# Expert weights of two MoE layers loaded in runs of 16 KB and 8 KB instead of 4 KB

## The chip, the cores and the metric

The kernel runs on one NeuronCore of a Trainium2 chip. Its time is the device time of one execution in microseconds (us). The kernel before was timed in 3 runs: 2659.59, 2661.01 and 2648.42 us, with a median of 2659.59.

A core has five engines that run side by side and wait for each other by semaphores: TensorE (PE, matmuls and transposes; its weight loads are shown as PEld), VectorE (DVE), ScalarE (ACT), GpSimd (POOL) and SyncE (SP), which here only issues transfers. Transfers between the device memory and the on-chip memory (SBUF, 128 partitions) are carried out by 16 DMA engines.

## The reference

Three blocks of a transformer run one after the other on x with 256 tokens and 1,024 features, all in fp32. The second has two layers, each ending in a mixture of experts; this is the part that the change touches:

```python
# in the block, for layer i; mc are the six conditioning vectors of the layer
    ... + mc[5] * ec_moe(modulate(rms_norm_2(hc, norm2_g[i]), mc[3], mc[4]), *moe)

def ec_moe(h, w_r, w_gate, w_up, w_down):
    ...
    aff = jax.nn.softmax(jnp.einsum("bnd,de->bne", h, w_r).astype(jnp.float32), axis=-1)
    gates, idx = lax.top_k(jnp.swapaxes(aff, 1, 2), cap)      # 32 tokens for each of 16 experts
    ...
    xs = h[bidx, idx]
    hid = jax.nn.silu(jnp.einsum("becd,edf->becf", xs, w_gate)) * jnp.einsum("becd,edf->becf", xs, w_up)
    ys = jnp.einsum("becf,efd->becd", hid, w_down) * gates[..., None].astype(h.dtype)
    return jnp.zeros_like(h).at[bidx, idx].add(ys)
```

The three matrices of an expert are 1024 x 1024, 4 MB each, so the two layers read 2 x 16 x 12 MB = 403 million bytes of expert weights, of 634 million that the kernel moves in all.

## The kernel before

All weights of the kernel pass through a ring of 6 slots of 16 KB per partition (`ring`, `RING = 6`). `weight_chunks` lists the chunks in the order of their use. SP takes the list in order: before it loads a chunk into a slot it waits until PE has used the chunk that was there, and each slot has a semaphore (`landed`) for PE to wait on.

An expert is six chunks of 2 MB: `g0 g1 u0 u1 d0 d1`, the upper and lower 512 rows of gate, up and down. In `rows_of` the 512 rows of a chunk are split as (k p): partition p gets rows p, 128 + p, 256 + p and 384 + p, each 4 KB long. A transfer is therefore 512 runs of 4 KB, four per partition.

Each MoE layer goes like this:
- Its input is normalised (`norm_act` for the first 128 tokens on ScalarE, `norm_dve` for the others on VectorE, lines L357 and L365) and stands in `xn`, tokens on partitions. PE turns it into `hT` for the router (L1519), and the 32 tokens of each expert are gathered out of `xn` by matmuls with one-hot columns (L1545), 128 features at a time, into `xsT` (128 features x tokens, 8 such tiles), where scale and shift are applied.
- A loop over expert pairs follows. For each expert PE waits for a slot, multiplies with the chunks of gate and up (L1571, 32 small matmuls on a chunk), ScalarE and VectorE make `hid` (L1504, L1475), PE transposes it (L1578), ScalarE copies it out (L1506), PE multiplies with the two down chunks (L1587), ScalarE copies the result to `ys` (L1508), and PE adds it to the output tokens by matmuls with the scatter matrix (L1594).
- In each matmul the feature (or hidden) number on the partitions of the small operand has to be the row number of the weights on the same partition.
- In SP's program the loads of expert 0 are issued ahead of the loop (L2175), as soon as their slots are free. `load_moe` then holds a loop over the others: `part` waits on `moe_used` for the slot and issues a 2 MB transfer whose expert number is in a register (L2191, L2193).

The vectors of the conditioning (`ada_w_2`) are computed as rows of 512 features and turned to columns, 128 features at a time, by `ada_columns_pe` (L816), 24 chunks in all; they and the gains of the norms (`cols`) are features on partitions.

Of the kernel before, what the change touches and what calls it, by code (L numbers as in the profile page):

```python
# [119 lines left out]
def offsets(table):  # L120
    at, out = 0, {}
    for name, n in table:
        out[name] = (at, n)
        at += n
    return out, at


COL_AT, N_COLS = offsets(COLS)
ROW_AT = [offsets(t) for t in ROWS]
N_ROWS = max(n for _, n in ROW_AT)  # L130

# [40 lines left out]
    return w[k0 * P:k1 * P, c0:c1].rearrange("(k p) n -> p k n", p=P)  # L172


def weight_chunks(A):


# [5 lines left out]
    def whole(name, w, k0, k1, c0, c1):  # L183
        chunk(name, k1 - k0, c1 - c0, (0, rows_of(w, k0, k1, c0, c1)))
# [26 lines left out]
    def moe(l):  # L211
        for e in range(N_EXPERTS):
            for what, w in (("g", "moe_w_gate_2"), ("u", "moe_w_up_2"), ("d", "moe_w_down_2")):
                for h in range(2):
                    whole(f"moe{l}_{e}{what}{h}", A[w][l, e], 4 * h, 4 * h + 4, 0, 1024)

    ev = A["ev_w_in_2"][0]
    whole("ev_kv", ev, 0, 8, 512, 768)
# [32 lines left out]
def program(nc, A, out, planned):  # L251
# [12 lines left out]
    with ctx:  # L264
# [37 lines left out]
        def constant(name, p=P):  # L302
            at, n = CONST_AT[name]
            return const[0:p, at:at + n]
# [43 lines left out]

        def norm_act(tag, ready):

            a = nc.scalar
            waits(a, *ready)
            a.activation(xn[:, 0, :], x[:, 0, :], ACT.Square, accum_out=stats[:, 0:1]).then_inc(*act_s.signals(f"{tag}.ss0"))  # L355
            a.wait_ge(*pool_s.after(f"{tag}.rstd0"))
            a.activation(xn[:, 0, :], x[:, 0, :], ACT.Copy, scale=stats[:, 4:5]).then_inc(*act_s.signals(f"{tag}.xn0"))  # L357

        def norm_dve(tag):
            v = nc.vector  # L360
            v.wait_ge(*dve_s.latest())
            v.tensor_tensor_reduce(out=xn[:, 1, :], in0=x[:, 1, :], in1=x[:, 1, :], scale=1.0, scalar=0.0,
                                   op0=ALU.mult, op1=ALU.add, accum_out=stats[:, 1:2]).then_inc(*dve_s.signals(f"{tag}.ss"))
            v.wait_ge(*pool_s.after(f"{tag}.rstd"))
            v.tensor_scalar(xn[:, 1, :], x[:, 1, :], stats[:, 5:6], None, ALU.mult).then_inc(*dve_s.signals(f"{tag}.xn1"))  # L365

        def normed(tag):
            return [(act_s, f"{tag}.xn0"), (dve_s, f"{tag}.xn1")]
# [441 lines left out]
        def ada_columns_pe(c):  # L810
            t_ = nc.tensor
            _, at, row_ = ada_place(c)
            t_.wait_ge(*act_s.after(f"ada.c{c}"))
            claim(at)
            for b in range(4):
                ins = t_.matmul(bank[at][:, 2 * b:2 * b + 2], row_[:, P * b:P * b + P], constant("ada_cols"),  # L816
                                start=True, stop=True, skip_group_check=True)
            ins.then_inc(*pe_s.signals(f"ada.e{c}"))
            lend(at, (dve_s, f"ada.m{c}"))
# [585 lines left out]

        def moe_pool(l):
            waits(nc.gpsimd, ((act_s, "ln silu"), (dve_s, "moe0.x3"))[l])
            nc.gpsimd.dma_start(w_r, A["moe_w_r_2"][l].rearrange("(k p) e -> p k e", p=P)).then_inc(s_side2["w_r"], 16)
            norm_pool(f"nmoe{l}")

        def moe_dve(l):
            v = nc.vector
            tag = f"moe{l}"
            norm_dve(f"nmoe{l}")
            turn_evac(f"h{tag}", h2_items[l], 1)

            v.memset(s_buf[:, 0, :], 0.0).then_inc(*dve_s.signals(f"{tag}.zeros"))
# [68 lines left out]
        def moe_act(l):  # L1486
            a = nc.scalar
            tag = f"moe{l}"
            norm_act(f"nmoe{l}", [(dve_s, ("ev_out1.x0", "sc_out1.x0")[l])])
            turn_evac(f"h{tag}", h2_items[l], 0)  # L1490
            a.wait_ge(*dve_s.after(f"{tag}.max"))
            for t in range(2):
# [17 lines left out]
        def moe_pe(l):  # L1510
# [39 lines left out]
            with t_.Fori(0, N_EXPERTS // 2) as i:  # L1550
                for b in range(2):
# [23 lines left out]
                    t_.wait_ge(moe_hid, done + 1)  # L1575
                    t_.wait_ge(moe_hTc, done)
                    for h in range(2):
                        ins = t_.transpose(bank[5][:, P * h:P * h + P], hid[b][:, P * h:P * h + P], ident)  # L1578
                    ins.then_inc(moe_hT, 1)
                    t_.wait_ge(moe_hTc, done + 1)  # L1580
                    t_.wait_ge(moe_yc, done)
# [590 lines left out]
        def load_plain(sp, name):  # L2172
            n, kt, width, pieces = chunks[name]
            for c0, src in pieces:
                sp.dma_start(slot(name)[:, :, c0:c0 + src.shape[2]], src).then_inc(landed[n % RING], 16)  # L2175
# [4 lines left out]
        def load_moe(sp, l):  # L2180

            parts = moe_parts(l)
            first = chunks[parts[0]][0]
            for c in range(RING):
                sp.wait_ge(*pe_s.after(f"used {names[first + c - RING]}"))
                load_plain(sp, parts[c])

            def part(c, i, expert):
                w = A[("moe_w_gate_2", "moe_w_up_2", "moe_w_down_2")[(c % 6) // 2]][l]
                s = (first + c) % RING  # L2190
                sp.wait_ge(moe_used, 12 * i + (96 * l + c + 1))  # L2191
                src = w[bass.ds(expert, 1), 512 * (c % 2):512 * (c % 2) + 512, :].rearrange("e (k p) n -> p (e k) n", p=P)
                sp.dma_start(ring[:, s, :].rearrange("p (k n) -> p k n", n=D), src).then_inc(landed[s], 16)  # L2193

            with sp.Fori(0, N_EXPERTS // 2 - 1) as i:
                for c in range(12):
                    part(c, i, 2 * i + (1 + c // 6))
            for c in range(6):
                part(c, N_EXPERTS // 2 - 1, N_EXPERTS - 1)
# [89 lines left out]
```

## Time and profile before

| | |
|---|---|
| median of 3 runs | 2659.59 us (2648.42 to 2661.01) |
| profiled execution: span from first to last instruction | 2661.3 us; the page names no time outside it |
| PE busy | 2127.6 us, 80% |
| DVE, ACT, POOL busy | 599.1, 342.2, 120.5 us |
| DMA | 634.34 MB, mean 238 GB/s |
| packets of SP's queue | 251,536, 623.83 MB |
| chain that ended last | PE 63%, DMA 28%, DVE 4% |

The profile is of one execution. Its page splits the span into 40 slices of 66.5 us and gives the busy share of each engine in tenths. The chain of waits goes back from the last instruction, at each step to what released it. A line like L1571 is a line of the kernel before. DMA share is the mean busy share of the 16 DMA engines; it can pass 1, because packets that follow each other on one engine overlap a little in the record.

### The profile page before, as it was taken

Reading aid. Unit: us, or ns where it says so; the run is one execution under the profiler, and the core shown is the slowest. Engines: PE = TensorE matmul, PEld = TensorE weight load, DVE = VectorE, ACT = ScalarE, POOL = GpSimd, SP = SyncE. Lnnn points to the kernel's source line nnn. Section 1 sums busy time; section 2 is a strip of 40 time slices with the busy share of each in tenths; the row PEclk is TensorE's granted clock in tenths of the full one; section 3 lists DMA queues with packets and bytes.
Section 4 is the critical chain, followed back from the end, with each engine's and each line's share of the span. In section 5 each row is a group of like instructions: output and inputs, shape, how many; then the busy total and the mean of one; then the engine's idle time right before and its main releaser. Section 6 shows DMA issues by size and latency. Waiting matters only on the chain.

```text
span 2661.3 us, 30350 instructions
## 1 busy us (share of the span) xinstructions
PE 2127.6 (80%) x12671; PEld 1258.4 (47%) x12671; DVE 599.1 (23%) x1662; ACT 342.2 (13%) x802; POOL 120.5 (5%) x154
## 2 busy tenths in 40 slices
PE   8999999898655555589855555549989999979999
PEld 3455545574322222267422222224558764446874
DVE  2223203673000000022300000012623421242330
ACT  1034211031000000010100000001311100211110
POOL 0100000530000000000000000001100000000000
PEclk9987699858888888889888888888979999959999
DMA  9767463301899999995299999996223434403430
GB/s 344 253 215 267 159 228 129 127 1 64 356 410 410 410 410 410 410 246 190 109 409 410 409 410 410 410 404 228 95 79 128 158 112 158 142 16 116 144 135 16
DMA packets 256024, 634.34 MB, mean 238 GB/s; under 512 B 7394, under 2 KB 89458, under 8 KB 255945
## 3 DMA queue, kind: packets, MB, share of 16 engines
q1 hardware_dynamic: 251536, 623.83, 62.7%
q0 software_dynamic: 1472, 5.76, 0.6%
q10 hardware_dynamic: 2936, 3.66, 0.4%
q8 instruction: 54, 0.88, 0.1%
q14 instruction: 26, 0.21, 0.0%
HBM read 632.13 MB, written 1.09 MB: 238 GB/s over the span
## 4 chain that ended last, share of the span: by engine, by line
PE 63%; DMA 28%; DVE 4%; SPq 2%; ACT 1%; issue 1%; POOL 1%; POOLq 0%; DVEq 0%; ACTq 0%
PE bank L538 20%; DMA ring<-in_moe_w_down 17%; PE bank L553 15%; DMA ring<-in_moe_w_gate 10%; PE bank L1909 6%; PE bank L596 3%; PE bank L618 3%; PE bank L1587 2%; PE bank L805 2%; SPq L2193 2%; PE bank L609 2%; PE bank L1571 2%; PE bank L464 1%; PE bank L1545 1%; PE bank L816 1%
## 5 line engine op out<-in xcount | busy, mean ns | idle before, releaser
L1571 PE MATMUL bank<-ring,arena 128*32 128x256 f32 x4096 | 306.4, 453 | 251.6 <-DMA ring<-in_moe_w_up 150.2
L553 PE MATMUL bank<-hT,ring 128*128 128x256 f32 x1920 | 423.2, 384 | 4.3 <-DVE arena L1950 3.0
L538 PE MATMUL bank<-ring,hT 128*128 128x512 f32 (+3 forms) x992 | 418.3, 581 | 8.8 <-DVE hT L490 3.8
L553 PEld LDWEIGHTS bank<-hT,ring 128*128 128x128 f32 x1920 | 370.0, 193 | 57.2 <-issue 6.1
L1571 PEld LDWEIGHTS bank<-ring,arena 128*32 128x32 f32 x4096 | 141.2, 126 | 401.9 <-DMA ring<-in_moe_w_up 187.3
L538 PEld LDWEIGHTS bank<-ring,hT 128*128 128x128 f32 x992 | 188.2, 194 | 226.8 <-issue 223.6
L1587 PE MATMUL bank<-ring,arena 128*32 128x256 f32 x2048 | 165.2, 479 | 108.9 <-DMA ring<-in_moe_w_down 107.9
L1587 PEld LDWEIGHTS bank<-ring,arena 128*32 128x32 f32 x2048 | 78.0, 133 | 182.3 <-DMA ring<-in_moe_w_down 102.6
L1909 PE MATMUL bank<-ring,arena 128*128 128x512 f32 x352 | 151.4, 592 | 0.0
L1475 DVE TENSOR_TENSOR arena<-arena,bank 128x256 f32<-128x256 f32 x32 | 13.5, 421 | 557.2 <-ACT arena L1504 557.2
L1909 PEld LDWEIGHTS bank<-ring,arena 128*128 128x128 f32 x352 | 66.9, 190 | 83.3 <-issue 83.2
L419 POOL TENSOR_SCALAR stats<-stats 128x1 f32<-128x1 f32 (+7 forms) x40 | 7.8, 195 | 2011.0 <-ACT xn L355 1400.3
L538 PE MATMUL bank<-ring,arena 128*128 128x512 f32 (+1 forms) x224 | 92.5, 574 | 1.1 <-DVE arena L488 1.1
L1504 ACT ACTIVATE arena<-bank 128x256 f32<-128x256 f32 x32 | 12.3, 383 | 594.1 <-PE bank L1571 594.1
L1473 DVE COPY arena<-bank 128x256 f32<-128x256 f32 x32 | 13.6, 424 | 321.9 <-PE bank L1563 321.7
L618 PE MATMUL bank<-arena,pT_buf 128*128 128x64 f32 (+1 forms) x408 | 82.4, 346 | 0.0
L618 PEld LDWEIGHTS bank<-arena,pT_buf 128*128 128x128 f32 x408 | 81.4, 278 | 0.4 <-ACT pT_buf L641 0.2
L1961 DVE TENSOR_SCALAR arena<-arena,cols 128x256 f32<-128x256 f32 x88 | 30.4, 408 | 204.7 <-ACT arena L1932 204.7
L596 PE MATMUL bank<-arena 64*128 64x256 f32 (+2 forms) x144 | 67.6, 595 | 5.9 <-DVE arena L1842 3.1
L1964 DVE SCALAR_TENSOR_TENSOR arena<-arena,cols 128x256 f32<-128x256 f32 x176 | 71.5, 477 | 0.0
L538 PEld LDWEIGHTS bank<-ring,arena 128*128 128x128 f32 x224 | 43.4, 195 | 48.6 <-issue 47.5
L805 PE MATMUL bank<-ring,rows 128*32 128x512 f32 x384 | 65.5, 817 | 0.0
(285 smaller groups left out, 1700.1 us busy)
## 6 DMA issues: line engine op xcount, KB each, us to landing
ring<-in_moe_w_gate SPq DMA_DIRECT2D x64, 2048.0 KB, 23.6
ring<-in_moe_w_up SPq DMA_DIRECT2D x64, 2048.0 KB, 23.8
ring<-in_moe_w_down SPq DMA_DIRECT2D x64, 2048.0 KB, 23.9
ring<-in_ada_w SPq DMA_DIRECT2D x24, 2048.0 KB, 8.5
ring<-in_w_up SPq DMA_DIRECT2D x44, 1024.0 KB, 6.9
ring<-in_w_in SPq DMA_DIRECT2D x11, 2048.0 KB, 9.3
ring<-in_w_down SPq DMA_DIRECT2D x10, 2048.0 KB, 7.8
ring<-in_w_out SPq DMA_DIRECT2D x6, 2048.0 KB, 8.2
```

The costliest lines, as they stand in the source:

```text
L538: ins = t_.matmul(bank[b][:, 0:n], lhsT(k)[:, P * t:P * t + P], w[:, k, c0:c0 + n], start=(k == 0), stop=(k == kt - 1))
L553: ins = t_.matmul(bank[b][:, 256 * (j % 2):256 * (j % 2) + 256], w[:, k, P * j:P * j + P], rhs[:, k, :], start=(k == 0), stop=(k == 7), sk ...
L596: t_.matmul(score_bank(i)[:, 0:u["keys"]], u["q"], u["k"], start=True, stop=True)\
L609: ins = t_.transpose(bank[6 + j % 2][0:n, P * k:P * k + P], p[:, P * k:P * k + n], ident)
L618: ins = t_.matmul(bank[j % 2][:, 0:v.shape[-1]], pT_buf[0:n, j % 2, P * k:P * k + P], v, start=(k == 0), stop=(k == len(u["v"]) - 1))
L805: ins = t_.matmul(bank[b][32 * j:32 * j + 32, :], spad[:, j + 4 * r, :], w[:, j + 4 * r, :], start=(r == 0), stop=(r == 1), skip_group_che ...
L1571: ins = t_.matmul(bank[4][32 * j:32 * j + 32, at:at + 256], xs_now[b][:, 4 * (c % 2) + k, :], w[:, k, 256 * j:256 * j + 256], start=(c % 2 ...
L1587: ins = t_.matmul(bank[6][32 * j:32 * j + 32, 0:256], hidT[b][:, f % 2, 32 * (f // 2):32 * (f // 2) + 32], w[:, k, 256 * j:256 * j + 256], ...
L1909: ins = t_.matmul(bank[b][:, :], actT[:, f, P * t:P * t + P], w[:, k, 512 * half:512 * half + 512], start=(f == 0), stop=(f == FF_TILES - 1))
L1961: ins = v.tensor_scalar(dst, src, w, col("conv_b_3", 44 * l + f), ALU.mult, ALU.add)
L1964: ins = v.scalar_tensor_tensor(out=dst, in0=src, scalar=w, in1=dst, op0=ALU.mult, op1=ALU.add)
L2193: sp.dma_start(ring[:, s, :].rearrange("p (k n) -> p k n", n=D), src).then_inc(landed[s], 16)
```

## The change

The runs in which expert weights are loaded get longer, and everything that is multiplied with them is numbered to match:
- A gate or up chunk is split as (p k) instead of (k p): partition p gets rows 4p to 4p + 3 of the 512, which lie side by side in memory, 16 KB. A down chunk is split as (j p r): partition p gets rows 2p and 2p + 1 of each 256, two runs of 8 KB.
- The norm ahead of a MoE layer writes `xn` with its features in the matching order, reading `x` in steps of 4 elements.
- The router's weights, the columns of norm2_g, and the conditioning vectors 3 and 4 (bias and computed value) take the same order. For the computed value, `ada_columns_pe` reads its row in steps of 4; for the others the order is set in the load or in the array of columns.
- The two halves of `hid` that are transposed are its even and odd columns instead of its left and right half.

```diff
+def expert_order(a):
+    return a.reshape(-1, 2, P, 4).transpose(0, 1, 3, 2).reshape(-1, P)
+
+def expert_rows(w, what):
+    if what == "d":
+        return w.rearrange("(j p r) n -> p j (r n)", j=2, r=2)
+    return w.rearrange("(p k) n -> p (k n)", k=4)
+
+def expert_slot(slot, what):
+    return slot.rearrange("p (j n) -> p j n", j=2) if what == "d" else slot
...
-                    whole(f"moe{l}_{e}{what}{h}", A[w][l, e], 4 * h, 4 * h + 4, 0, 1024)
+                    chunk(f"moe{l}_{e}{what}{h}", 4, 1024, (None, expert_rows(A[w][l, e, 512 * h:512 * h + 512], what)))
...
+        def in_order(buf, t, experts):
+            if not experts:
+                return buf[:, t, :]
+            return buf[:, t, :].rearrange("p (h q k) -> p h k q", h=2, k=4)
+
+        def in_tiles(buf, t, experts):
+            return buf[:, t, :].rearrange("p (h k q) -> p h k q", h=2, k=4) if experts else buf[:, t, :]
...
-            a.activation(xn[:, 0, :], x[:, 0, :], ACT.Copy, scale=stats[:, 4:5]).then_inc(*act_s.signals(f"{tag}.xn0"))
+            a.activation(in_tiles(xn, 0, experts), in_order(x, 0, experts), ACT.Copy, scale=stats[:, 4:5]).then_inc(*act_s.signals(f"{tag}.xn0"))
...
-            v.tensor_scalar(xn[:, 1, :], x[:, 1, :], stats[:, 5:6], None, ALU.mult).then_inc(*dve_s.signals(f"{tag}.xn1"))
+            v.tensor_scalar(in_tiles(xn, 1, experts), in_order(x, 1, experts), stats[:, 5:6], None, ALU.mult).then_inc(*dve_s.signals(f"{tag}.xn1"))
...
-                ins = t_.matmul(bank[at][:, 2 * b:2 * b + 2], row_[:, P * b:P * b + P], constant("ada_cols"),
+                of = row_[:, b:512:4] if c % 12 // 2 in (3, 4) else row_[:, P * b:P * b + P]
+                ins = t_.matmul(bank[at][:, 2 * b:2 * b + 2], of, constant("ada_cols"),
...
-            nc.gpsimd.dma_start(w_r, A["moe_w_r_2"][l].rearrange("(k p) e -> p k e", p=P)).then_inc(s_side2["w_r"], 16)
+            nc.gpsimd.dma_start(w_r.rearrange("p (h k) e -> p h k e", h=2), A["moe_w_r_2"][l].rearrange("(h p k) e -> p h k e", h=2, k=4)).then_inc(s_side2["w_r"], 16)
...
-                        ins = t_.transpose(bank[5][:, P * h:P * h + P], hid[b][:, P * h:P * h + P], ident)
+                        ins = t_.transpose(bank[5][:, P * h:P * h + P], hid[b][:, h:256:2], ident)
...
-                src = w[bass.ds(expert, 1), 512 * (c % 2):512 * (c % 2) + 512, :].rearrange("e (k p) n -> p (e k) n", p=P)
-                sp.dma_start(ring[:, s, :].rearrange("p (k n) -> p k n", n=D), src).then_inc(landed[s], 16)
+                src = w[bass.ds(expert, 1), 512 * (c % 2):512 * (c % 2) + 512, :]
+                if what == "d":
+                    src = src.rearrange("e (j p r) n -> p (e j) (r n)", j=2, r=2)
+                else:
+                    src = src.rearrange("e (p k) n -> p (e k n)", k=4)
+                sp.dma_start(expert_slot(ring[:, s, :], what), src).then_inc(landed[s], 16)
```

No instruction changes its place on any engine: each engine issues the same number of the same operations in the same order, and only their access patterns differ. On SP, in the loop over the experts, the transfers of the first expert of a pair stood like this before (partitions x runs x elements):

```order
L2193 DMA ring<-in_moe_w_gate 128x4x1024
L2191 REGISTER_ALU
L2193 DMA ring<-in_moe_w_up 128x4x1024
L2191 REGISTER_ALU
L2193 DMA ring<-in_moe_w_down 128x4x1024
```

And in the changed kernel:

```order
L2238 DMA ring<-in_moe_w_gate 128x4096
L2232 REGISTER_ALU
L2238 DMA ring<-in_moe_w_up 128x4096
L2232 REGISTER_ALU
L2238 DMA ring<-in_moe_w_down 128x2x2048
```

Nothing moved; four runs of 1,024 elements per partition have become one of 4,096, or two of 2,048.

## Rows read from the trace of the kernel before

**Rows 1.** The page's 40 slices: PE, the DMA engines, and GB/s.

```profile
PE   8999999898655555589855555549989999979999
DMA  9767463301899999995299999996223434403430
GB/s 344 253 215 267 159 228 129 127 1 64 356 410 410 410 410 410 410 246 190 109 409 410 409 410 410 410 404 228 95 79 128 158 112 158 142 16 116 144 135 16
```

**Rows 2.** Stretches: length, busy us (xcount) of PE, PEld, DVE, ACT, POOL; PEclk, DMA share, GB/s.

```profile
672.39:1137.01 464.62, 266.26 (x3306) 127.61 (x3298) 20.67 (x79) 27.00 (x54) 0.00 (x0) 0.84 1.02 408
1316.31:1781.17 464.86, 254.85 (x3306) 122.98 (x3298) 20.67 (x79) 26.99 (x54) 0.00 (x0) 0.89 1.02 408
1785.00:1800.00 15.00, 0.00 (x0) 0.00 (x0) 10.83 (x15) 3.45 (x5) 4.45 (x10) 0.65 1.05 387
1140.00:1150.00 10.00, 5.57 (x52) 4.52 (x48) 6.49 (x10) 1.83 (x4) 0.92 (x3) 0.96 1.10 288
30.00:40.00 10.00, 10.00 (x24) 3.64 (x24) 1.59 (x5) 1.17 (x2) 0.00 (x0) 1.00 1.09 352
```

**Rows 3.** The chain that ended last, in the first loop: start us, us, what.

```profile
737.64 3.28 PE bank L1587 x32
...
744.63 23.69 DMA ring<-in_moe_w_down
768.36 3.27 PE bank L1587 x32
```

**Rows 4.** PE's waits, 672.39 to 1137.01: us in total, times, longest us.

```profile
PE bank L1571 <- DMA ring<-in_moe_w_up: 76.9, 30, 3.4
PE bank L1587 <- DMA ring<-in_moe_w_down: 52.0, 29, 3.1
PE bank L1571 <- DMA ring<-in_moe_w_gate: 42.1, 14, 3.0
PE bank L1578 <- DVE arena L1475: 15.1, 16, 1.0
```

**Rows 5.** DMA queues (packets, MB, share), and issues (KB each, us to landing).

```profile
q1 hardware_dynamic: 251536, 623.83, 62.7%
q8 instruction: 54, 0.88, 0.1%
...
ring<-in_moe_w_gate SPq DMA_DIRECT2D x64, 2048.0 KB, 23.6
```

**Rows 6.** Timeline of the second loop: start us, us, engine, line, operation [idle before <-releaser].

```profile
1366.49 3.42 PE L1571 MATMUL bank<-ring,arena 128*32 128x256 f32 x32 [3.19 <-DMA ring<-in_moe_w_up]
...
1371.61 1.93 PE L1571 MATMUL bank<-ring,arena 128*32 128x256 f32 x32 [1.70 <-DMA ring<-in_moe_w_up]
...
1374.97 0.38 ACT L1506 ACTIVATE arena<-bank 128x256 f32<-128x256 f32 x1 [0.98 <-PE bank L1578]
1376.73 3.42 PE L1587 MATMUL bank<-ring,arena 128*32 128x256 f32 x32 [1.79 <-DMA ring<-in_moe_w_down]
```

**Rows 7.** Timeline of SP at the start of the first loop.

```profile
672.39 2.08 SPq L2193 DMA_DIRECT2D ring<-in_moe_w_gate  x2
...
698.73 9.75 SPq L2193 DMA_DIRECT2D ring<-in_moe_w_up  x2
```

**Rows 8.** Single lines: duration ns min/median/max, first and last start us.

```profile
L1578 PEld LDWEIGHTS bank<-const,arena x64: 137/141/144, 678.3 to 1773.9; 128*128 128x128 f32 x64
...
L816 PEld LDWEIGHTS bank<-const,arena x192: 186/192/338, 92.5 to 388.5; 128*128 128x128 f32 x192
...
L365 DVE TENSOR_SCALAR xn<-x_sb,stats x10: 752/752/754, 11.7 to 2422.4; 128x1024 f32<-128x1024 f32 x10
...
L362 DVE CUSTOM_DVE_ANT_0 xn<-x_sb x10: 1224/1225/1226, 5.8 to 2420.2; 128x1024 f32<-128x1024 f32 x10
```

**Rows 9.** Timeline of the norm ahead of the first MoE layer.

```profile
627.06 1.15 ACT L357 ACTIVATE xn<-x_sb,stats 128x1024 f32<-128x1024 f32 x1 [0.97 <-POOL stats L422]
...
630.15 1.04 PE L445 MATMUL bank<-const,xn 128*128 128x128 f32 x8
```

More of the change, by code:

```diff
@@ L128, with columns @@
 COL_AT, N_COLS = offsets(COLS)
+def expert_order(a):
+    return a.reshape(-1, 2, P, 4).transpose(0, 1, 3, 2).reshape(-1, P)
+def columns(name, a):
+    a = np.asarray(a)
+    if name == "norm2_g_2":
+        return expert_order(a)
+    if name == "ada_b_2":
+        b = a.reshape(2, 6, D)
+        return np.concatenate([expert_order(b[l, v]) if v in (3, 4) else b[l, v].reshape(-1, P) for l in range(2) for v in range(6)])
+    return a.reshape(-1, P)
 ROW_AT = [offsets(t) for t in ROWS]
@@ L347, in lend, with norm_act @@
             freed[b] = marks
-        def norm_act(tag, ready):
+        def in_order(buf, t, experts):
[4 more added lines that the diff above has]
+            return buf[:, t, :].rearrange("p (h k q) -> p h k q", h=2, k=4) if experts else buf[:, t, :]
+        def norm_act(tag, ready, experts=False):
             a = nc.scalar
@@ L356, in norm_act, with norm_dve @@
             a.wait_ge(*pool_s.after(f"{tag}.rstd0"))
-            a.activation(xn[:, 0, :], x[:, 0, :], ACT.Copy, scale=stats[:, 4:5]).then_inc(*act_s.signals(f"{tag}.xn0"))
-        def norm_dve(tag):
+            a.activation(in_tiles(xn, 0, experts), in_order(x, 0, experts), ACT.Copy, scale=stats[:, 4:5]).then_inc(*act_s.signals(f"{tag}.xn0"))
+        def norm_dve(tag, experts=False):
             v = nc.vector
@@ L1413, in moe_dve @@
             tag = f"moe{l}"
-            norm_dve(f"nmoe{l}")
+            norm_dve(f"nmoe{l}", experts=True)
             turn_evac(f"h{tag}", h2_items[l], 1)
@@ L1488, in moe_act @@
             tag = f"moe{l}"
-            norm_act(f"nmoe{l}", [(dve_s, ("ev_out1.x0", "sc_out1.x0")[l])])
+            norm_act(f"nmoe{l}", [(dve_s, ("ev_out1.x0", "sc_out1.x0")[l])], experts=True)
             turn_evac(f"h{tag}", h2_items[l], 0)
@@ L2185, in load_moe @@
                 sp.wait_ge(*pe_s.after(f"used {names[first + c - RING]}"))
-                load_plain(sp, parts[c])
+                _, _, _, ((_, src),) = chunks[parts[c]]
+                s = (first + c) % RING
+                sp.dma_start(expert_slot(ring[:, s, :], "gud"[c // 2]), src).then_inc(landed[s], 16)
             def part(c, i, expert):
+                what = "gud"[(c % 6) // 2]
                 w = A[("moe_w_gate_2", "moe_w_up_2", "moe_w_down_2")[(c % 6) // 2]][l]
@@ L2274 @@
     arrays["onehots"] = onehots()
-    arrays["cols"] = np.ascontiguousarray(np.concatenate([np.asarray(inputs[n]).reshape(-1, P) for n, _ in COLS]).T)
+    arrays["cols"] = np.ascontiguousarray(np.concatenate([columns(n, inputs[n]) for n, _ in COLS]).T)
     for i, table in enumerate(ROWS):
```

## The prediction

> **What bounds the kernel now.** I started with the slices of the page: DMA stands at 9 and about 410 GB/s in two long stretches, while PE falls to 5, the lowest of the whole span [rows 1]. Then I measured those stretches. From 672.39 to 1137.01 us and from 1316.31 to 1781.17 us the DMA engines are busy all the time (share 1.02, since neighbouring packets overlap a little) and PE is busy for 266 and 255 of 465 us [rows 2]. These are the expert loops of the two MoE layers. The chain of waits has one pattern through them: about 24 us of a down load, 3.28 us of matmuls on it, a few short steps, then the next load [rows 3]; two loads that end alike lie 737.64 to 768.36 = 30.72 us apart, one expert. An expert is six loads of 2 MB, so one load takes 30.72 / 6 = 5.12 us. The waits of PE say the same: in the first loop 76.9 + 52.0 + 42.1 = 171 us for loads, and 15.1 us for the largest of all others [rows 4]. A load lands about 24 us after its issue, 4.6 loads at that pace, so the queue never runs dry.
>
> So 90 loads (experts 1 to 15; those of expert 0 are already there when the loop starts) set the length of each loop: 90 x 5.12 = 460.8 of its 464.6 and 464.9 us. The remaining 3.8 us are the start of the queue. What a load costs is the whole question.
>
> **What a load costs.** A packet is one contiguous run. The hardware queue of SP counts 251,536 packets [rows 5]. The rows that the 345 loads and stores of that queue name in the code (512 for each of the 192 expert loads, 1,024 for each of the 24 ada loads, 1,024 for each of the 44 up loads, 1,024 for each of the 24 sc pieces, and so on through the list) add up to 246,016, and 16 a transfer, one per engine, add 5,520: together exactly 251,536. No run was put together with another, and none was longer than 4 KB.
>
> The saturated stretches of other loads then give time against run length, per engine (a sixteenth of the rate) [rows 2]:
> - 4 KB runs: 32 per engine and load in 5.12 us, 160.0 ns each (410 GB/s).
> - 2 KB runs (diff weights, 1785 to 1800): 387 / 16 = 24.2 bytes per ns, 84.7 ns each.
> - From the two: 75.3 ns per 2 KB, and 160.0 - 150.6 = 9.4 ns that don't depend on the length.
> - The line is tested by two points it wasn't made from. 512-byte runs (sc weights, 1140 to 1150) should take 28.2 ns, 290 GB/s; the row has 288. 1 KB runs (the cmp weights, mixed with 2 KB ones, 30 to 40) should give 348 or a bit more; the row has 352.
>
> Run on to 8 KB the line gives 310.6 ns, to 16 KB 611.8 ns.
>
> **The change, part by part.**
> - Gate and up: 8 runs of 16 KB per engine instead of 32 of 4 KB, 8 x 611.8 = 4.894 us a load, 0.226 less. On the path stand 15 experts x 4 x 2 layers = 120 of them: 27.1 us.
> - Down: 16 runs of 8 KB, 4.970 us, 0.150 less, 60 loads: 9.0 us. Together 36.1 us, with an expert at 29.52 instead of 30.72 us. Bounds: nothing, if a run gains no more beyond 4 KB (all rows end there), and 180 x 32 x 9.4 ns = 54 us, if nearly all the fixed part went, which needs runs longer than these; so 0 to 36.1 by the mechanism, and I take 36.1, since four lengths lie on the line.
> - PE doesn't take over: the 171 us of waits for loads [rows 4] must pay 18 us per loop. What is late next is the load again. A part's matmuls take 3.42 us at the slower pace and 1.93 at the faster [rows 6], both below 4.89.
> - SP: the same instructions in the same order. Its issues come in pairs of 2.1 us while the queue is empty and take 9.7 us a pair once it is full [rows 7]; nobody waits for them, because 24 us of loads lie ahead. Shorter lists can only free SP earlier.
> - The transposes of hid (L1578) read every second column. The 64 weight loads take 141 ns now [rows 8]. They stand between the last up part and the first down part, where the copy ends at 1374.97 + 0.38 = 1375.35 and the down load lands only for 1376.73 [rows 6]: 1.4 us of cover, 1.2 after the change. If their time doubled it would cost 0.3 us an expert, hidden; the first expert of each layer has no cover, 0.6 us at worst. I take 0.
> - Norm before each MoE: x is read every fourth element. VectorE's half takes 0.752 us and PE waits for it [rows 8]; the same 1,024 elements take 1.225 us in the square sum before it, one element at a time. I take that for the strided read, +0.47 x 2 = 0.9 us. Bounds: 0, if the step doesn't matter to it, and 2 x (2 x 1.225 - 0.752) = 3.4 us if every element cost double; it can't be quicker than the plain read. ScalarE's half (1.147 us) ends at 628.21, and its transposes start behind other matmuls at 630.15 [rows 9]: 1.9 us of cover, so 0 even if doubled.
> - Ada columns: in 8 of 24 chunks the weight operand is read with step 4. That is 64 weight loads of 192 ns [rows 8]; 0 to 12.3 us (doubled, all on the path). No row shows the weight operand read in steps; the ones there are, of many tiles, stay near 192 ns, so I take 0 and keep the 12.3 for the range.
> - The router's weights come in 256-byte runs instead of 64-byte ones, on POOL's queue, far ahead of their use: 0. The columns of norm2_g and ada_b are permuted outside the chip: 0.
>
> Sum: the profiled execution has a span of 2661.3 us, and the page gives it no time outside that; it lies 0.06% above the median of 2659.6. 2661.3 - 36.1 + 0.9 = 2626.1; from the median, 2624.4. I say 2625.
>
> A rule weighed. "DMA: Bandwidth & Descriptors" in the Trainium skill (section Bandwidth, Measured) lists 425 GB/s as the highest rate of a very large load. No row here comes near it; by it an expert would take 29.6 us instead of 29.52, and the sum would come out 2 to 3 us higher. The same page (section SWDGE vs HWDGE vs iDMA) has a packet preferably at 4096 B or less; that it would keep a long run from paying off is the first rival below.
>
> The Trainium skill's page "Advanced Engine Details and Errata" (section Memory Cachelines) says that reads which each touch another 16-byte line are slower. A step of four fp32 is just that; I found no row here that shows such an SBUF read. It speaks against the norm and the ada term, and would put them nearer to 3 and 12 us than to 0.9 and 0.
>
> **Rivals.**
> - *The long runs are cut.* If the queue cuts a run at 4 KB, or pays 9.4 ns for each 4 KB whatever the run, the loads stay at 5.12 us and only the strided reads are left: 2659.6 + 0.9 = 2660.5 us. For it: no row of SP's queue shows a packet above 4 KB. Against it: the instruction queue moved 0.88 MB in 54 packets, 16.3 KB each [rows 5], so the engines do move such packets; and no shorter run was gathered up to 4 KB either. If it is cut at 8 KB, all 180 loads save 0.150: 27 us, 2633.5.
> - *Slower: memory is read in places further apart.* The rows of neighbouring partitions lay 4 KB apart in memory, now 16 KB (8 KB for down), so what the 16 engines read at one moment lies four times (twice) as far apart. If that makes memory the limit, every load is longer. The nearest slower rate is that of the 2 KB runs, 387 GB/s: 5.42 us a load, 180 x 0.30 = +54 us, 2714. It decides from the point where a load takes more than 5.12 us. Against it: at all four run lengths the rate is what the engines' line gives, so memory has not yet shown a limit of its own. "DMA: Bandwidth & Descriptors" (section Latency and other measured facts) in the Trainium skill tells of rates that fall when rows lie 2 MB or more apart, and not at 512 KB; the rows here lie 16 KB apart, so by that rule nothing falls.
> - *The strided reads eat part of it*: 12 us of ada and 3 of norm leave 36 - 15 = 21, 2639.
>
> **How the numbers follow.** The forecast 0.70, with its own range 2612 to 2637 (runs of the same kernel lie between 2648 and 2661). The gain in part, by a cut at 8 KB or by strided reads, 0.10. No gain 0.12. Slower 0.06. More than forecast 0.02. The range reaches from 2608 to 2646 and leaves out the last three, 2 in 10. About half a per cent, 13 us, can be told from no change: faster 0.81, same 0.13, slower 0.06.
>
> **What would show it.** The packet count of SP's queue at 251,536 - 98,304 + 128 x 128 + 64 x 256 = 186,000; if it stands at 251,536 the runs were cut. About 426 GB/s with a share near 1.01 in the loops; equal points of the chain 29.5 us apart; each loop near 446.5 us; VectorE's norm half at 1.2 us in two of ten places. The prediction is wrong if a load takes 5.12 us or more, or if PE's waits for loads vanish.

## The result and the profile after

| | us | ratio to before, 95% interval |
|---|---|---|
| before, 14 runs beside the changed kernel | 2659.32 (2648.42 to 2678.22) | |
| after, 14 runs | 2647.15 (2632.33 to 2654.62) | 0.9945 [0.9927, 0.9962] |
| after in a second set, 12 runs (before there 2660.48) | 2643.59 (2621.04 to 2658.03) | 0.9941 [0.9914, 0.9969] |

The change makes the kernel 12 us faster by the medians and about 15 by the ratio (10 to 19 by its interval), where 34 were forecast. The time lies just above the range of 2608 to 2646. The profiled execution of after has a span of 2636.9 us, 24.4 less than that of before.

First the page of the changed kernel, which answers [rows 1] and [rows 5]: the slices, the queue of SP, and the time from issue to landing.

```profile
PE   7999999988856555689865565649989999979999
PEclk9976799967887888789888878779979999959999
DMA  9756644301599999995299999995224335403430
GB/s 343 252 207 224 223 175 153 134 26 65 232 426 426 426 427 426 427 267 192 109 427 426 426 427 427 426 410 203 76 80 159 132 109 181 137 1 126 143 130 16
...
q1 hardware_dynamic: 186000, 623.83, 61.2%
...
ring<-in_moe_w_gate SPq DMA_DIRECT2D x64, 2048.0 KB, 26.6
```

The packet count is the forecast one to the packet, so each run of 16 or 8 KB is one packet, and the plateaus stand at 426 GB/s instead of 410. Easily passed over are the slices ahead of the plateaus, where expert weights play no part: the fourth has 224 GB/s instead of 267, the fifth 223 instead of 159, the sixth 175 instead of 228, while PE stays at 9. The same transfers fall at other times, so ahead of the loops the kernel already doesn't keep the pace of before.

Next the chain of waits in the first loop, which answers [rows 3]. One expert is 927.68 - 898.16 = 29.52 us, and again 957.19 - 927.68 = 29.51 (before 30.72; forecast 29.52).

```profile
898.16 3.57 PE bank L1625 x32
...
901.75 25.89 DMA ring<-in_moe_w_down
...
927.68 1.98 PE bank L1625 x32
...
957.19 1.98 PE bank L1625 x32
```

PE's waits in the first loop of after answer [rows 4]. The three waits for loads are 66.3 + 40.8 + 37.4 = 144.5 us instead of 171: smaller, but still far above all others, so the loads remain the bound.

```profile
PE bank L1609 <- DMA ring<-in_moe_w_up: 66.3, 30, 3.0
PE bank L1609 <- DMA ring<-in_moe_w_gate: 40.8, 22, 3.0
PE bank L1625 <- DMA ring<-in_moe_w_down: 37.4, 21, 2.9
PE bank L1616 <- DVE arena L1513: 15.3, 16, 1.0
```

To see where the time went, the span is cut at four points that both kernels have: the first gate/up matmul of each expert loop and the last down matmul of each. The columns are those of [rows 2]. First before:

```profile
0.00:670.23 670.23, 626.34 (x2382) 356.18 (x2382) 234.00 (x722) 141.82 (x370) 83.19 (x100) 0.85 0.50 177
670.23:1140.37 470.14, 271.73 (x3375) 130.31 (x3374) 21.14 (x81) 27.00 (x54) 0.00 (x0) 0.84 1.02 405
1140.37:1314.13 173.76, 156.55 (x612) 114.41 (x612) 49.81 (x109) 20.25 (x37) 4.21 (x9) 0.90 0.52 161
1314.13:1783.15 469.02, 258.97 (x3375) 125.25 (x3374) 21.09 (x80) 26.99 (x54) 0.00 (x0) 0.89 1.02 406
1783.15:2656.13 872.98, 813.97 (x2930) 532.22 (x2930) 272.40 (x670) 126.14 (x287) 33.09 (x45) 0.93 0.36 121
```

And the changed kernel:

```profile
0.00:685.52 685.52, 639.26 (x2382) 365.99 (x2382) 234.71 (x722) 143.13 (x370) 82.98 (x100) 0.85 0.49 173
685.52:1138.13 452.61, 279.22 (x3375) 131.91 (x3374) 21.16 (x81) 27.03 (x54) 0.00 (x0) 0.82 1.00 421
1138.13:1307.44 169.31, 152.85 (x613) 113.19 (x612) 50.21 (x109) 21.26 (x37) 3.87 (x9) 0.92 0.54 165
1307.44:1758.33 450.89, 278.40 (x3375) 131.73 (x3374) 21.12 (x80) 27.03 (x54) 0.00 (x0) 0.83 1.00 422
1758.33:2631.71 873.38, 815.85 (x2931) 533.10 (x2930) 272.46 (x670) 126.21 (x287) 33.10 (x45) 0.93 0.36 121
```

The two loops give 17.5 + 18.1 = 35.7 us, against 36.1 forecast. The stretch between them gives 4.4 more, at a granted clock of 0.92 instead of 0.90; that this comes from the change isn't shown, because kernels further down with loads in 4 KB rows have it too (170.14 and 170.18 us instead of 173.76). And the stretch in front of the first loop, in which no expert weight is waited for, takes 15.3 us more. Together -35.7 - 4.4 + 15.3 + 0.4 = -24.4, the difference of the spans.

In the front stretch the instruction that changed is the ada column matmul. Its weight loads in one of the eight chunks that are now read in steps (one line's rows from 185 to 188 us: duration in ns, min/median/max), before:

```profile
L816 PEld LDWEIGHTS bank<-const,arena x8: 192/192/193, 185.9 to 186.7; 128*128 128x128 f32 x8
```

and after:

```profile
L854 PEld LDWEIGHTS bank<-const,arena x8: 309/329/329, 185.6 to 187.2; 128*128 128x128 f32 x8
```

A weight load of 192 ns has become one of 329. On PE's timeline the group of eight matmuls takes 1.97 us instead of 1.00, and what stands behind it starts that much later. Before:

```profile
185.98 1.00 PE L816 MATMUL bank<-const,arena 128*128 128x2 f32 x8
186.91 0.48 PE L596 MATMUL bank<-xn 64*128 64x128 f32 x2
```

After:

```profile
185.66 1.97 PE L854 MATMUL bank<-const,arena 128*128 128x2 f32 x8
187.57 0.48 PE L633 MATMUL bank<-xn 64*128 64x128 f32 x2
```

Eight chunks at 0.97 us are 7.8 us. Not every chunk pays that price. A plain chunk that falls into a stretch at half the clock (granted clock 0.50) is slow already. This one of before takes 1.84 us for its eight matmuls, with weight loads of up to 338 ns:

```profile
165.10 1.84 PE L816 MATMUL bank<-const,arena 128*128 128x2 f32 x8 [0.74 <-ACT arena L824]
```

A stepped chunk of after at the same clock (198.61) takes 1.95, with loads of 330 ns, so there the step costs 0.1 us. In this execution of before, one of the eight chunks in question stood at half clock (1.81 us at 291.17). The eight take 15.6 us after and 8.9 before on PE's timeline: 6.8 us more.

The other 7.5 to 8.5 of the 15.3 are not in any instruction that changed. From 165 to 360 us, the attention of layer 0 with the ada chunks woven in, PE is busy for 193.5 us or more of 195 in both, and the granted clock differs, 0.74 before and 0.71 after:

```profile
165.00:360.00 195.00, 193.53 (x903) 109.68 (x904) 53.22 (x337) 60.77 (x215) 0.00 (x0) 0.74 0.61 213
```

```profile
165.00:360.00 195.00, 193.62 (x863) 111.91 (x864) 53.01 (x336) 59.64 (x213) 0.00 (x0) 0.71 0.58 205
```

Clock time missing from full speed: 195 x 0.26 = 50.7 us before and 195 x 0.29 = 56.6 after, 6 us more. With two digits of the clock that is good to about 2 us.

### The profile page after: what moved, and what is told of

Same layout as the page of the kernel before. It is cut to its first block, busy times and chain, and to the rows that moved or that the text cites. A ratio compares the mean times of both kernels' runs of the same rounds, so it can differ in the third digit from the quotient of the medians.

```text
span 2636.9 us, 30350 instructions
## 1 busy us (share of the span) xinstructions
PE 2165.6 (82%) x12671; PEld 1275.9 (48%) x12671; DVE 600.4 (23%) x1662; ACT 344.7 (13%) x802; POOL 120.0 (5%) x154
## 3 DMA queue, kind: packets, MB, share of 16 engines
q1 hardware_dynamic: 186000, 623.83, 61.2%
## 4 chain that ended last, share of the span: by engine, by line
PE 62%; DMA 30%; DVE 4%; ACT 1%; issue 1%; POOL 1%; SPq 0%; POOLq 0%; DVEq 0%; ACTq 0%
DMA ring<-in_moe_w_down 30%; PE bank L575 20%; PE bank L590 15%; PE bank L1947 6%; PE bank L1625 3%; PE bank L633 3%; PE bank L655 3%; PE bank L842 2%; PE bank L646 2%; PE bank L501 1%; PE bank L1583 1%; PE bank L854 1%; DVE arena L1311 1%; PE bank L1609 1%; PE bank L1557 1%
## 5 line engine op out<-in xcount | busy, mean ns | idle before, releaser
L1609 PE MATMUL bank<-ring,arena 128*32 128x256 f32 x4096 | 318.8, 466 | 211.5 <-DMA ring<-in_moe_w_up 132.8
L1625 PE MATMUL bank<-ring,arena 128*32 128x256 f32 x2048 | 171.4, 493 | 86.0 <-DMA ring<-in_moe_w_down 77.1
L1542 ACT ACTIVATE arena<-bank 128x256 f32<-128x256 f32 x32 | 12.3, 384 | 571.4 <-PE bank L1609 571.4
```

Source lines behind the costliest of these rows:

```text
L1609: ins = t_.matmul(bank[4][32 * j:32 * j + 32, at:at + 256], xs_now[b][:, 4 * (c % 2) + k, :], w[:, k, 256 * j:256 * j + 256], start=(c % 2 ...
L1625: ins = t_.matmul(bank[6][32 * j:32 * j + 32, 0:256], hidT[b][:, f % 2, 32 * (f // 2):32 * (f // 2) + 32], w[:, k, 256 * j:256 * j + 256], ...
```

## The experiments

The theory after the profile of the changed kernel (A): the loads do just what was forecast; the stepped read of the ada weight operand takes back 8 us by itself and about as much again by TensorE's clock. The rivals: the norm or the hid transposes carry a part of the loss, or the front stretch was merely unlucky in that one execution. Every time below is the median of a set of runs beside runs of before on the same chip. Before's own medians there were 2663.24, 2659.44 and 2660.48 us.

### Loads alone, and steps alone

`loads_only` keeps the long runs and reads every operand as before (ada, norm and hid each back to their old form):

```diff
-                of = row_[:, b:512:4] if c % 12 // 2 in (3, 4) else row_[:, P * b:P * b + P]
+                of = row_[:, P * b:P * b + P]
...
-            norm_dve(f"nmoe{l}", experts=True)
+            norm_dve(f"nmoe{l}")
...
-            norm_act(f"nmoe{l}", [(dve_s, ("ev_out1.x0", "sc_out1.x0")[l])], experts=True)
+            norm_act(f"nmoe{l}", [(dve_s, ("ev_out1.x0", "sc_out1.x0")[l])])
...
-                        ins = t_.transpose(bank[5][:, P * h:P * h + P], hid[b][:, h:256:2], ident)
+                        ins = t_.transpose(bank[5][:, P * h:P * h + P], hid[b][:, P * h:P * h + P], ident)
```

> The long runs of the changed kernel with every operand read as in the kernel before (features and weights are then multiplied in different orders, so the values are not the reference's; the work is the same). Theory A, the loads give all of the 36 us and the stepped reads ahead of the loops take the rest back: 2659.3 - 36 = about 2623 us, ratio 0.986, first loop entered at about 670 us as before. Theory B, the loads themselves give less than the trace of one execution says (a lower clock in the loops, or a loss behind them): 2640 to 2647 us, ratio 0.993 to 0.996, as the changed kernel.

Measured: 2619.11 us (2609.41 to 2640.31, 6 runs), 0.9838 [0.9799, 0.9876]. That is 44 us below before in that set (33 to 54), a bit more than the 36 of the loops alone. The windows of its profile, front and the first loop:

```profile
0.00:669.58 669.58, 625.90 (x2382) 354.08 (x2382) 233.93 (x722) 141.87 (x370) 82.98 (x100) 0.85 0.50 178
669.58:1120.38 450.80, 274.77 (x3375) 129.06 (x3374) 21.18 (x81) 26.99 (x54) 0.00 (x0) 0.83 1.00 421
```

The front is that of before to 0.7 us, the loop that of after.

`steps_only` is the mirror image: all stepped reads, loads in 4 KB rows.

```diff
 def expert_rows(w, what):
-    if what == "d":
-        return w.rearrange("(j p r) n -> p j (r n)", j=2, r=2)
-    return w.rearrange("(p k) n -> p (k n)", k=4)
+    return w.rearrange("(k p) n -> p k n", p=P)
...
```

> The stepped reads of the changed kernel (ada, norm, hid) with the loads in 4 KB runs as before (values not the reference's for the same reason; same work). Theory A: slower, +9 us if only the longer weight loads count (8 chunks x 0.97 us and 2 x 0.4 us of the norm), +20 if a lower clock in the attention stretch comes with them: 2668 to 2680 us. Theory B: 2659 to 2663 us.

Measured: 2683.67 us (2669.47 to 2692.37, 12 runs), 1.0073 [1.0046, 1.0101], 20 us slower than before. In its profiled execution, one of the shorter ones (2674.06), the front is 683.39 us and the loops are 468.99 and 470.34. The loss sits in the steps and outside the loops.

### Which of the steps

The ada read alone, on the kernel before:

```diff
-                ins = t_.matmul(bank[at][:, 2 * b:2 * b + 2], row_[:, P * b:P * b + P], constant("ada_cols"),
+                ins = t_.matmul(bank[at][:, 2 * b:2 * b + 2], row_[:, b:512:4] if c % 12 // 2 in (3, 4) else row_[:, P * b:P * b + P], constant("ada_cols"),
```

> The kernel before with the stepped read of the ada rows alone, in 8 of 24 chunks (two of the conditioning vectors then come out permuted; same work). Theory A: nearly all of what the stepped reads cost together is here, +8 to +20 us, 2667 to 2679; the granted clock between 175 and 350 us lower than before, and 64 weight loads of about 330 ns. Theory B: no change, within 3 us.

Measured: 2669.96 us (2663.91 to 2683.8, 12 runs), 1.0026 [1.0004, 1.0048]: 7 us slower (1 to 13), the least that any kernel with this read showed. Its profiled execution, with a front of 690.84 us and a granted clock of 0.67 from 165 to 360, was one of the two longest of the twelve (2683.74). Eight of the twelve took 2664 to 2672 us, about what the step's own time adds to before (2663.24 + 7.8 = 2671). So that profile isn't typical of this kernel.

The norm alone (with loads in 4 KB rows; shown against the kernel before):

```diff
-            norm_dve(f"nmoe{l}")
+            norm_dve(f"nmoe{l}", experts=True)
...
-            norm_act(f"nmoe{l}", [(dve_s, ("ev_out1.x0", "sc_out1.x0")[l])])
+            norm_act(f"nmoe{l}", [(dve_s, ("ev_out1.x0", "sc_out1.x0")[l])], experts=True)
```

> Loads in 4 KB rows, ada columns and hid read as before (so the features of the ada coefficients and of hid stand in another order than the reference's); only the norm ahead of the experts reads x every fourth element, in both layers. Theory: VectorE's half goes from 0.75 to 1.13 us twice, ScalarE's from 1.15 to 2.13 us twice and is covered: +0.8 us, no difference that can be measured (2663 to 2665). Rival: the norm carries the 12 us that lie between all stepped reads together (+20) and the ada read alone (+7): +12 us, 2675. The profile tells it by the stretch between the end of attention and the first expert matmul.

Measured: 2666.16 us (2641.32 to 2680.78, 12 runs), 1.003 [1.0002, 1.0058]: 7 us slower by the median, with an interval from 0.5 to 15. By the time alone the rival could not be excluded. The profile contradicts it: front 666.45 us, 4 less than before, and between the loops 170.14. That execution took 2674.34, and what is long in it is the stretch behind the second loop (see below), which reads nothing in steps. The two halves of the norm, VectorE's and ScalarE's (ns min/median/max; the max is the stepped one, twice of ten):

```profile
L400 DVE TENSOR_SCALAR xn<-x_sb,stats x10: 752/754/1132, 12.0 to 2433.7; 128x1024 f32<-128x1024 f32 x10
...
L392 ACT ACTIVATE xn<-x_sb,stats x10: 1147/1148/2143, 11.1 to 2426.8; 128x1024 f32<-128x1024 f32 x10
```

The part on the path is 2 x (1.132 - 0.754) = 0.8 us.

The transposes of hid alone (with loads in 4 KB rows):

```diff
-                        ins = t_.transpose(bank[5][:, P * h:P * h + P], hid[b][:, P * h:P * h + P], ident)
+                        ins = t_.transpose(bank[5][:, P * h:P * h + P], hid[b][:, h:256:2], ident)
```

> Loads in 4 KB rows, ada and norm read as before (features in another order than the reference's); only the transposes of hid read every second column. Theory: 64 weight loads go from 141 to 206 ns each, all but those of the first expert of each layer lie under a load: within 0.5 us of before. Rival: they are on the path in every expert (0.13 us x 32 = 4 us), or they carry the 12 us that the ada read alone leaves open: +4 to +12 us, with the expert loops 2 to 6 us longer each.

Measured: 2661.24 us (2640.05 to 2671.28, 12 runs), 1.0005 [0.9981, 1.0028]. Nothing, as forecast, although the weight loads do get longer (141 ns in [rows 8]):

```profile
L1614 PEld LDWEIGHTS bank<-const,arena x64: 194/206/219, 674.8 to 1770.3; 128*128 128x128 f32 x64
```

### Is it the steps, or any time on TensorE there?

`ada_twice` has no steps. It issues the same four column matmuls a second time in the same eight chunks of the kernel before:

```diff
-            for b in range(4):
-                ins = t_.matmul(bank[at][:, 2 * b:2 * b + 2], row_[:, P * b:P * b + P], constant("ada_cols"),
-                                start=True, stop=True, skip_group_check=True)
+            for again in range(2 if c % 12 // 2 in (3, 4) else 1):
+                for b in range(4):
+                    ins = t_.matmul(bank[at][:, 2 * b:2 * b + 2], row_[:, P * b:P * b + P], constant("ada_cols"),
+                                    start=True, stop=True, skip_group_check=True)
```

> Before, with the four ada column matmuls (and their weight loads of 192 ns, no steps anywhere) issued twice in the 8 chunks that the change reads in steps. This adds 8 x about 1.0 us to TensorE in the same places as the stepped read (8 x 1.1 us). Theory (time on TensorE's path, whatever makes it): +8 us direct, like the stepped read alone (+7), 2671, and the granted clock of the attention stretch no other than the spread of the kernel before. Rival 1: added time there is given back by the clock or by waits: 0, 2663. Rival 2: the stepped read does more than its own time, by the clock: then this kernel gains or loses its 8 us alone while the stepped ones lose 13 to 20.

Measured: 2683.06 us (2678.67 to 2695.62, 6 runs), 1.0101 [1.007, 1.0133]: 24 us slower (19 to 35 by the interval), not 8. The expectation was wrong, and in the telling direction: ordinary matmuls, 0.9 us more in a chunk (the first of the eight takes 1.98 us for its 16, where before took 1.00 for 8), cost two to three times their own duration. The profile has 19.3 us more in front than before and the same loops:

```profile
0.00:689.51 689.51, 645.29 (x2445) 369.79 (x2445) 234.39 (x722) 141.71 (x370) 83.19 (x100) 0.84 0.49 172
165.00:360.00 195.00, 193.62 (x901) 113.64 (x902) 53.35 (x336) 58.39 (x210) 0.00 (x0) 0.68 0.55 194
```

Clock time missing from 165 to 360: 195 x 0.32 = 62.4, 12 more than before; with 8 x 0.9 = 7 us of its own work that is the 19 (summed over the eight chunks, one of them at half clock, its own work is 8.0 us). So the loss beyond the own time doesn't need stepped reads: ordinary matmuls in this stretch show it too. That it comes with any further work there is not shown, and most runs of `ada_steps_only` speak against it.

### The ada order without a stepped weight read

Here the eight chunks read the weight operand in order again. ScalarE, which copies the row out of PSUM anyway, reads PSUM in steps of 4 and so writes the row in the permuted order:

```diff
-                of = row_[:, b:512:4] if c % 12 // 2 in (3, 4) else row_[:, P * b:P * b + P]
+                of = row_[:, P * b:P * b + P]
...
-            nc.scalar.activation(at, bank[b][:, :], ACT.Copy).then_inc(*act_s.signals(f"ada.c{c}"))
+            src = bank[b][:, :]
+            if c % 12 // 2 in (3, 4):
+                at, src = at.rearrange("p (k q) -> p k q", k=4), src.rearrange("p (q k) -> p k q", k=4)
+            nc.scalar.activation(at, src, ACT.Copy).then_inc(*act_s.signals(f"ada.c{c}"))
```

> The changed kernel, but ScalarE sets the order of the 8 ada chunks while it copies the row out of PSUM (steps of 4 on the PSUM side), so PE reads its weights in one piece. Theory A: the whole gain but 1 us comes back, 2623 to 2626 us. Theory B: 2640 to 2647 as the changed kernel. If the stepped PSUM read costs ScalarE the same 1.9 times as its read of x does, a copy takes 1.1 instead of 0.6 us, and up to 4 us are lost.

Measured: 2625.52 us (2619.72 to 2643.46, 6 runs), 0.9878 [0.9841, 0.9914]. The copies take what they took before; all 24 lie between 572 and 600 ns, the eight stepped ones included:

```profile
L865 ACT ACTIVATE arena<-bank x24: 572/597/600, 63.2 to 372.4; 128x512 f32<-128x512 f32 x24
```

This kernel beats both others. Since it and the changed kernel had been timed in different sets, both were run again side by side, and with them the long runs plus the stepped ada read alone.

> The changed kernel once more, beside the others of this set on one chip. As before: two groups of times, about 2638 and 2652, median 2647 (ratio 0.9945), which is 18 us more than with the ada columns ordered by ScalarE.

> The changed kernel with plain weight reads for ada, the same kernel as the first time: median 2624 to 2627 (ratio 0.988), groups about 2622 and 2642. Theory: below the changed kernel by 9 us of direct weight load time and what TensorE's clock adds to it, 15 to 22 us in all. Rival: they were 22 us apart only because they ran in different sets, and lie within 5 us here.

And `loads_ada_steps`, shown against `loads_only`:

```diff
-                of = row_[:, P * b:P * b + P]
+                of = row_[:, b:512:4] if c % 12 // 2 in (3, 4) else row_[:, P * b:P * b + P]
```

> Long runs for the loads and the stepped ada read, nothing else stepped (norm and hid read as before, so hid's features stand in another order than the reference's). Theory: the ada read carries the whole difference between the long runs alone (2619) and the changed kernel (2647): within 4 us of the changed kernel in this set, 2643 to 2650. Rival: norm and hid carry a part, as the sum of the single parts with 4 KB loads says (ada +7, norm +7, hid +1): then this is at 2626 to 2635, midway.

| one set | us | ratio to before | front | 165 to 360: clock |
|---|---|---|---|---|
| before (19 runs) | 2660.48 | | 670.2 (its first profile) | 0.74 |
| after_again (12) | 2643.59 | 0.9941 [0.9914, 0.9969] | 686.9 | 0.70 |
| loads_ada_steps (8) | 2648.14 | 0.9943 [0.9914, 0.9972] | 681.9 | 0.72 |
| ada_by_act_again (6) | 2622.19 | 0.9874 [0.9841, 0.9906] | 670.4 | 0.76 |

The kernel with nothing stepped but ada stands where the changed kernel stands, and taking the stepped ada read out of the changed kernel gives 21 us. That settles it for the ada read on long runs. The windows of the second execution of each, after and the ordered copy:

```profile
0.00:686.94 686.94, 640.53 (x2381) 365.87 (x2381) 234.70 (x722) 142.98 (x370) 83.01 (x100) 0.84 0.49 173
```

```profile
0.00:670.39 670.39, 626.15 (x2381) 355.13 (x2381) 234.31 (x722) 142.73 (x370) 82.99 (x100) 0.85 0.50 177
```

Over all profiles, the five with the ada read in steps of 4 have fronts of 681.9 to 690.8 us, and `ada_twice` has 689.5. The seven with the plain read lie between 666.5 and 673.5. The granted clock from 165 to 360 us is 0.67 to 0.72 in those six and 0.72 to 0.77 in these seven: the groups of the clock touch, those of the fronts don't.

### Another step, and a step on the other side

Half the step, on the kernel before:

```diff
-                ins = t_.matmul(bank[at][:, 2 * b:2 * b + 2], row_[:, P * b:P * b + P], constant("ada_cols"),
+                ins = t_.matmul(bank[at][:, 2 * b:2 * b + 2], row_[:, 256 * (b // 2) + b % 2:256 * (b // 2) + 256:2] if c % 12 // 2 in (3, 4) else row_[:, P * b:P * b + P], constant("ada_cols"),
```

> Before, with the ada weight operand read with step 2 instead of 4 in the 8 chunks (another order of the columns than the reference's). One look for the duration of a weight load. If the price goes by how far apart the elements lie (as hid's: 141 to 206 ns with step 2), they take some 260 ns instead of 192, against 329 with step 4: 64 x 0.07 = 4.4 us. If two elements in a 16-byte line are enough for full speed, they stay at 192 and hid's 206 has another cause.

Measured, in a single run: 2654.77 us, a front of 662.2 us, and in the same chunk as above

```profile
L816 PEld LDWEIGHTS bank<-const,arena x8: 196/197/198, 185.5 to 186.3; 128*128 128x128 f32 x8
```

So step 2 costs this load 5 ns, step 4 costs it 137. Both stepped forms of hid and ada with step 2 come out near 200 ns. What is fast in hid is its plain load of 141; why that is quicker than ada's plain 192 was not looked into.

Finally the norm with its step on the other side, x read in order and xn written in steps of 128 elements, on top of the ordered ada copy:

```diff
-            return buf[:, t, :].rearrange("p (h q k) -> p h k q", h=2, k=4)
+            return buf[:, t, :].rearrange("p (h q k) -> p h q k", h=2, k=4)
...
-            return buf[:, t, :].rearrange("p (h k q) -> p h k q", h=2, k=4) if experts else buf[:, t, :]
+            return buf[:, t, :].rearrange("p (h k q) -> p h q k", h=2, k=4) if experts else buf[:, t, :]
```

> The changed kernel with plain weight reads for ada (ScalarE's copy out of PSUM sets the order), and the norm reads x in order and writes xn in steps instead. If only stepped reads of SBUF cost, VectorE's half is back at 0.75 us and ScalarE's at 1.15: at most 0.8 us less than with the ordered ada read alone, 2625, a difference that can't be measured by the time but by the rows. If stepped writes cost as much, the halves stay at 1.13 and 2.13 us and the time is the same. Its operands otherwise are those of the changed kernel, hid's stepped transposes included.

Measured: 2623.79 us (2620.27 to 2645.44, 5 runs), 0.9869 [0.9835, 0.9903], no better than the ordered ada copy alone. The stepped halves take 1.20 to 1.23 us on VectorE and 2.08 on ScalarE, against 1.13 and 2.14 with stepped reads: a step on the writing side costs as much.

## Why the prediction was wrong

**What held.** The bound (the loads, in both loops), the packet law made from four run lengths (29.52 us an expert forecast, 29.51 measured; 426 GB/s), the count of 186,000 packets, and the gain in the loops: 36.1 forecast, 35.7 measured. The rivals of cut runs and of slow memory were shown false by the same rows. The norm was forecast at 0.9 us and measured at 0.8; its ScalarE half went to 2.13 us, and its cover held with 1 us to spare. Hid at 0 held in its own experiment.

**The step that failed** is "Ada columns: ... so I take 0 and keep the 12.3 for the range". It was mis-sized twice.
- *Its own time.* The rows that I leant on, weight loads "of many tiles" near 192 ns, were all reads in order. They said nothing of a step of four, and were no ground for the low end of a range from 0 to 12.3. The measured time on TensorE is 8 x 0.97 = 7.8 us at full clock (6.8 between the two profiled executions), inside the bound. The Trainium skill's "Advanced Engine Details and Errata" (Memory Cachelines) spoke against this very term; I quoted it and took 0. By that rule a read whose every element lies on another 16-byte line is slow and two on one line are enough for full speed: step 4 with 329 ns against 192, and step 2 with 197, agree with it. The weight loads of hid don't: with step 2, two elements on a line, they went from 141 to 206 ns.
- *What it sets off.* The bound of 12.3 us counted the duration and held TensorE's clock fixed. In this stretch PE is busy nearly all the time, and the granted clock moves between its full 2.4 GHz and half of that (1.00 and 0.50 around single chunks). In the profiled executions more work on PE went with a lower mean clock (0.74, 0.71, 0.68 for before, after, `ada_twice`), and the work around it took longer too. That the added work lowers the clock is argued from this and not shown. The 15.3 us of the first profile, 16.7 of the second, and 19.3 with ordinary matmuls are all about twice the added work or more. An upper end of some 25 us would have held all of them.

With this term as measured, the forecast would have been 2625 + 15 = 2640, inside the range. The rival "the strided reads eat part of it" gave 2639 and came nearest to the true case; I gave it, together with the cut at 8 KB, only 0.10. That its number fits is in part luck: its 12 us of ada were doubled weight loads alone and its norm 3 us, where the runs had 7 to 8 us of weight loads, about as much again with the lower clock, and 0.8 us of norm.

**What stays open.** Four to seven microseconds lie between 2640 and the two medians of after. The times of one kernel spread over 17 to 40 us, and in some sets they fall in two groups (`loads_only`: five runs at 2609 to 2621 us and one at 2640). Part of the spread is the stretch behind the second loop, which takes 873 to 875 us in eleven of the profiles and 889 to 892 in three (`norm_steps_only`, `loads_ada_steps`, `norm_by_writes`). The 100 us in which they differ, 100 us into that stretch, here from the long runs with the stepped ada read:

```profile
1854.00:1954.00 100.00, 92.43 (x308) 60.62 (x308) 42.10 (x156) 30.73 (x109) 6.07 (x4) 0.66 0.11 37
```

and from the ordered copy:

```profile
1841.20:1941.20 100.00, 92.61 (x355) 55.94 (x353) 44.24 (x160) 33.45 (x112) 7.80 (x6) 0.86 0.20 63
```

Of the 26 runs of after 14 lie above 2645 us; of the two kernels without the stepped ada read on long runs (`loads_only` and the ordered copy, three sets) 4 in 18 lie at 2640 to 2643, 12 us or more above the others. Whether the later arrival at that stretch causes it was not shown. Two of the three profiles with the long stretch have the plain ada read and fronts of 666.45 and 673.47 us, so it doesn't take a late arrival; `ada_twice` arrives as late as after and has one long run in six. It also stays open why the stepped ada read cost only 7 us (1 to 13) on top of 4 KB loads and some 21 to 28 on top of long ones. In most runs of the kernel with 4 KB loads the part beyond the step's own time was missing. And that more work is the cause of the lower clock rests on six slower fronts against eight, one execution each, not on an experiment that sets the clock.

## What to carry to other kernels

A bound for added TensorE time in a dense stretch must leave room for the clock: here 8 us of work on PE came with fronts 12 to 21 us longer in six profiled executions, though one set of twelve runs lost only 7 us. When a layout change needs a permutation somewhere, put the step into ScalarE's read of PSUM (free here, 597 ns with and without) or under a load, and not into a weight operand on the critical path. A row of the same operation with another access pattern isn't a near row: between ends of 0 and 12 us, with no row of the pattern, the middle is the honest value, and a rule that speaks against the low end should move it.

## What the runs showed of the hardware

- Loads by SP's queue keep the same fixed part per packet up to 16 KB: expert loads of 2 MB took 30.72 / 6 = 5.12 us in 4 KB packets, and 29.51 / 6 = 4.92 us with 16 KB and 8 KB ones (4.92 by the line from 512-byte to 4 KB packets). No packet was cut.
- A 128 x 128 fp32 weight load read with step 4 took 329 ns instead of 192, with step 2 it took 197; hid's went from 141 to 206 with step 2. Where the granted clock was 0.50, the plain load took 333 and the one with step 4 took 330.
- 1,024 fp32 elements per partition read with step 4: VectorE 0.754 to 1.132 us, ScalarE 1.147 to 2.13. Written with step 128: 1.20 to 1.23 and 2.08.
